# Attention of a two-layer block: values stationary in two column halves, row sums inverted, spread and multiplied across three steps of the next tile

## The reference

```python
s_win = jnp.einsum('bnqgrd,bnkgd->bngrqk', qb, kw).astype(jnp.float32) * scale
s_win = jnp.where(valid[None, :, None, None], s_win, NEG_INF)
s_ctx = jnp.einsum('bnqgrd,bcgd->bngrqc', qb, k_ctx).astype(jnp.float32) * scale
p = jax.nn.softmax(jnp.concatenate([s_win, s_ctx, s_sink], axis=-1), axis=-1).astype(v.dtype)
o = (jnp.einsum('bngrqk,bnkgd->bnqgrd', p[..., :kw_len], vw)
     + jnp.einsum('bngrqc,bcgd->bnqgrd', p[..., kw_len:-1], v_ctx))
...
x = x + g1 * (jnp.concatenate([att, ret, cnv], axis=-1) @ w_out[l])
```

## Time and profile before

| | us |
|---|---|
| median of 3 runs | 1916.67 (1910.70 to 1926.17) |
| the profiled execution, device time | 1919.19 |
| its span, first to last instruction | 1917.4 |
| PE busy, share of the span | 1822.6, 95% |
| DVE / ACT / POOL busy | 1339.3 / 1050.9 / 119.9 |
| DMA | 472.85 MB, mean 247 GB/s |
| mean granted TensorE clock | 0.982 |

### The profile page before, as it was taken

How to read it: one execution, slowest core, us unless ns; L and a number is a source line. 1 busy time by engine, 2 the same in 40 slices (tenths; PEclk the granted TensorE clock), 3 DMA queues, 4 the chain that set the end, 5 groups by cost and what they waited for, 6 DMA issues and landing times.

```text
span 1917.4 us, 23772 instructions
## 1 busy us (share of the span) xinstructions
PE 1822.6 (95%) x8964; PEld 1480.7 (77%) x8964; DVE 1339.3 (70%) x1280; ACT 1050.9 (55%) x1009; POOL 119.9 (6%) x126
## 2 busy tenths in 40 slices
PE   4999899999999999987999999999999999999996
PEld 2986578888888888576888788888888888888885
DVE  2579645333323367756888888889888898898886
ACT  3334644322222153545777776777776776777774
POOL 1123600000000012400000000000000000000000
PEclk8999989999999999997999999999999999999999
DMA  8325823532342234735999999999999999999994
GB/s 291 126 88 207 303 75 78 140 96 86 95 109 83 74 97 132 258 138 175 370 332 354 358 340 345 368 346 354 369 328 362 351 361 359 338 354 352 353 367 154
DMA packets 245911, 472.85 MB, mean 247 GB/s; under 512 B 10546, under 2 KB 60564, under 8 KB 245804
## 3 DMA queue, kind: packets, MB, share of 16 engines
q1 hardware_dynamic: 241712, 468.14, 68.9%
q10 hardware_dynamic: 4092, 3.20, 0.6%
HBM read 470.26 MB, written 1.05 MB: 246 GB/s over the span
## 4 chain that ended last, share of the span: by engine, by line
PE 48%; DMA 21%; DVE 16%; ACT 8%; issue 5%; POOL 2%; SPq 0%; DVEq 0%; ACTq 0%; POOLq 0%
PE bank L543 13%; PE bank L545 13%; PE bank L544 13%; DMA raw<-in_moe_w_gate_dram 10%; DVE parts L1707 9%; ACT parts L1409 6%; DMA raw<-in_moe_w_down_dram 5%; DMA raw<-in_moe_w_up_dram 4%; DMA raw<-in_ada_w_dram 2%; PE bank L561 1%; PE bank L1047 1%; POOL gb L1663 1%; DVE parts L1692 1%; PE bank L790 1%; DVE ACC L2180 1%
## 5 line engine op out<-in xcount | busy, mean ns | idle before, releaser
L1707 DVE TENSOR_TENSOR parts<-raw,parts 128x2048 fp32r<-128x2048 f32 x336 | 764.9, 2289 | 115.0 <-ACT parts L1409 113.9
L1409 ACT ACTIVATE parts<-raw 128x2048 fp32r<-128x2048 f32 x336 | 642.7, 1919 | 260.4 <-DMA raw<-in_moe_w_up_dram 94.9
L543 PE MATMUL bank<-parts,XEr 128*128 128x512 f32 x896 | 357.2, 399 | 8.7 <-DVE parts L1707 6.3
L545 PE MATMUL bank<-parts,XEr 128*128 128x512 f32 x896 | 350.1, 391 | 0.0
L544 PE MATMUL bank<-parts,XEr 128*128 128x512 f32 x896 | 349.4, 390 | 0.0
L1270 ACT ACTIVATE parts<-raw 128x2048 fp32r<-128x2048 f32 (+1 forms) x62 | 113.2, 1831 | 270.2 <-PE bank L545 250.0
L1692 DVE TENSOR_TENSOR parts<-raw,parts 128x2048 fp32r<-128x2048 f32 (+1 forms) x62 | 135.8, 2194 | 138.2 <-ACT parts L1270 137.9
L543 PEld LDWEIGHTS bank<-parts,XEr 128*128 128x128 f32 x896 | 168.7, 188 | 49.9 <-DVE parts L1707 10.3
L545 PEld LDWEIGHTS bank<-parts,XEr 128*128 128x128 f32 x896 | 168.5, 188 | 36.6
L544 PEld LDWEIGHTS bank<-parts,XEr 128*128 128x128 f32 x896 | 168.9, 188 | 32.6
L543 PE MATMUL bank<-parts,HTr 128*128 128x512 f32 x448 | 175.6, 392 | 1.3 <-DVE HTr L1707 0.8
(11 more groups left out here) (245 smaller groups left out, 2289.7 us busy)
## 6 DMA issues: line engine op xcount, KB each, us to landing
raw<-in_moe_w_gate_dram SPq DMA_DIRECT2D x112, 1024.0 KB, 7.2
raw<-in_moe_w_up_dram SPq DMA_DIRECT2D x112, 1024.0 KB, 7.2
raw<-in_moe_w_down_dram SPq DMA_DIRECT2D x112, 1024.0 KB, 6.7
raw<-in_ada_w_dram SPq DMA_DIRECT2D x28, 1024.0 KB, 8.0
more<-in_ada_w_dram SPq DMA_DIRECT2D x20, 1024.0 KB, 7.7
raw<-in_w_in_dram SPq DMA_DIRECT2D x12, 1024.0 KB, 5.1
raw<-in_ffn_w_gate_dram SPq DMA_DIRECT2D x22, 512.0 KB, 4.0
raw<-in_ffn_w_up_dram SPq DMA_DIRECT2D x22, 512.0 KB, 5.4
```

The source lines that it names most:

```text
L543: nc.tensor.matmul(out, st[0], mv[0], start=start, stop=False)
L545: return nc.tensor.matmul(out, st[1], mv[0], start=False, stop=stop)
L1409: nc.scalar.activation(parts[:, n % PARTS, 0, :], raw[:, r, :], ACT.Copy).then_inc(hi_ready, 1)
L1707: return nc.vector.tensor_tensor(out, a, b, op)
```

## The change

- `values`: the values (64 columns of group g) are stationary and write to the partitions 64g to 64g+63 of OB; the turned probabilities are moving (128 columns). The two groups alternate. The result is feature-major: no turn of the attended tile is needed, and `turn_attended` is gone.
- The row sums: VectorE adds the sink and inverts (`invert_sums`) in the next tile's step m % 4 == 0, and for the last tile at the top of step `last`. TensorE spreads them over 64 partitions a group (`spread_sums`, 8 matmuls against the identity) at the top of step m % 4 == 1. ScalarE copies that bank to `proj` (`sums_out`). VectorE multiplies OB by it (`normalise`) at the top of step m % 4 == 2, the last tile's at the end.
- In steps m % 4 == 2 the modulation products run ahead of the values.
- ScalarE and VectorE read the attended tile from `proj` for the high and low parts.
- The first half of each w_out item group is loaded with its rows permuted, as two loads of 64 partitions.

```diff
@@ loads
-                for k0, k1 in HALVES:
-                    split_item([cols(io["w_out"][layer], h * SLICE, (h + 1) * SLICE, k0, k1)],
-                               k1 - k0, SLICE, n % 2, (n + layer) % 2)
+                w = io["w_out"][layer][:, h * SLICE:(h + 1) * SLICE]
+                groups = [w[256 * g:256 * g + 256, :].rearrange("(r p) n -> p r n", p=HEAD_DIM) for g in range(KV_HEADS)]
+                split_item(groups, KT // 2, SLICE, n % 2, (n + layer) % 2)
@@ TensorE
+            def spread_sums(layer, i):
+                t = order_of(layer)[i]
+                mixed[layer, t, 0] = len(mixed) + 1
+                b = open_a(("sums", layer, t))
+                after(recip_ready)
+                turn = i % 2
+                for r in range(4):
+                    for g in range(KV_HEADS):
+                        head = g * 4 + r
+                        mm = nc.tensor.matmul(b[64 * g:64 * g + 64, r * P:(r + 1) * P],
+                                              rsum[:, turn, head:head + 1].broadcast_to([P, HEAD_DIM]), ident, start=True, stop=True)
+                mm.then_inc(a_full, 1)
...
-                    for kb in range(first, NT):
-                        mm = nc.tensor.matmul(OB[:, head * 64:(head + 1) * 64], PT[:, n % 4, kb * P:(kb + 1) * P],
-                                              proj[:, kb, C_V + 64 * g:C_V + 64 * g + 64],
-                                              start=(kb == first), stop=(kb == NT - 1))
+                    for kb in range(first, NT):
+                        for g in range(KV_HEADS):
+                            mm = nc.tensor.matmul(OB[64 * g:64 * g + 64, r * P:(r + 1) * P], proj[:, kb, C_V + 64 * g:C_V + 64 * g + 64],
+                                                  PT[:, (2 * m + g) % 4, kb * P:(kb + 1) * P],
+                                                  start=(kb == first), stop=(kb == NT - 1))
...
                 for m in range(last + 2):
+                    if m % 4 == 1 and m >= 5:
+                        spread_sums(layer, m // 4 - 1)
                     if m < last:
                         scores(2 * m)
                         scores(2 * m + 1)
...
                     if m >= 2:
-                        values(2 * m - 4)
-                        values(2 * m - 3)
-                    if m % 4 == 2 and 6 <= m < last:
-                        turn_attended(layer, order_of(layer)[m // 4 - 1])
-                    if m < last:
+                        if m % 4 == 2 and m < last:
+                            for _ in range(ADA_ITEMS[layer][m]):
+                                ada_product()
+                        values(m - 2)
+                    if m < last and m % 4 != 2:
                         for _ in range(ADA_ITEMS[layer][m]):
                             ada_product()
@@ ScalarE
+            def attended_high(layer, i):
+                t = order_of(layer)[i]
+                act.wait_ge(att_read, evacuated(layer, i))
+                nc.scalar.activation(hTr[:, 0, 0:4, t * P:(t + 1) * P],
+                                     proj[:, t, C_Q:C_RQ].rearrange("p (k n) -> p k n", k=4), ACT.Copy).then_inc(mix_hi, 1)
...
+                    if m % 4 == 1 and m >= 5:
+                        sums_out(m // 4 - 1)
...
+                sums_out(last // 4 - 1)
@@ VectorE
+                def invert_sums(i):
+                    after(esink_ready)
+                    sums = rsum[:, i % 2, :]
+                    step(tt(sums, sums, esink[:, i % 2, :], ALU.add))
+                    nc.vector.reciprocal(sums, sums).then_inc(recip_ready, 1)
+
+                def normalise(i):
+                    tile = order_of(layer)[i]
+                    dve.wait_ge(att_done, base + 8 * i + 8)
+                    dve.wait_ge(a_done, job[("sums", layer, tile)] + 1)
+                    tt(proj[:, tile, C_Q:C_RQ], OB[:, :], proj[:, tile, C_Q:C_RQ], ALU.mult).then_inc(att_read, 1)
...
                 for m in range(last + 2):
+                    if m % 4 == 2 and 6 <= m < last:
+                        normalise(m // 4 - 1)
+                    if m == last:
+                        invert_sums(m // 4 - 1)
...
+                        if m % 4 == 0 and m:
+                            invert_sums(m // 4 - 1)
...
-                    if m % 4 == 1 and m >= 5:
-                        turn = (m // 4 - 1) % 2
-                        tile = order_of(layer)[m // 4 - 1]
-                        after(esink_ready)
-                        step(tt(rsum[:, turn, :], rsum[:, turn, :], esink[:, turn, :], ALU.add))
-                        step(nc.vector.reciprocal(rsum[:, turn, :], rsum[:, turn, :]))
-                        dve.wait_ge(att_done, base + 2 * m - 2)
-                        tt(proj[:, tile, C_Q:C_RQ].rearrange("p (h d) -> p h d", d=HEAD_DIM), OB[:, :].rearrange("p (h d) -> p h d", d=HEAD_DIM),
-                           per_group(rsum[:, turn, :], HEAD_DIM), ALU.mult).then_inc(att_read, 1)
+                    if m == last + 1:
+                        normalise(last // 4 - 1)
```

More of the change, by code:

```diff
@@ L368, in order_of, with evacuated @@
             return (2, 3, 0, 1) if layer == 0 else (0, 1)
+        def evacuated(layer, i):
+            return layer * (NT + 1) + i + 2
         def attention_of(layer):
@@ L780, in turn, with values @@
                     mm.then_inc(a_full, 1)
[L782 to L785, removed]
+                def values(m):
+                    t, r, _ = its[2 * m]
+                    if m % 4 == 0 and m:
                         after(att_read)
-                    pe.wait_ge(a_done, job[("probs", layer, n)] + 1)
                     first = 0 if t < TT else TT
+                    pe.wait_ge(a_done, job[("probs", layer, 2 * m + 1)] + 1)
                     for kb in range(first, NT):
-                        mm = nc.tensor.matmul(OB[:, head * 64:(head + 1) * 64], PT[:, n % 4, kb * P:(kb + 1) * P],
-                                              proj[:, kb, C_V + 64 * g:C_V + 64 * g + 64],
-                                              start=(kb == first), stop=(kb == NT - 1))
-                    mm.then_inc(att_done, 1)
+                        for g in range(KV_HEADS):
+                            mm = nc.tensor.matmul(OB[64 * g:64 * g + 64, r * P:(r + 1) * P], proj[:, kb, C_V + 64 * g:C_V + 64 * g + 64],
+                                                  PT[:, (2 * m + g) % 4, kb * P:(kb + 1) * P],
+                                                  start=(kb == first), stop=(kb == NT - 1))
+                            if kb == NT - 1:
+                                mm.then_inc(att_done, 1)
                 last = len(its) // 2
                 for m in range(last + 2):
+                    if m % 4 == 1 and m >= 5:
+                        spread_sums(layer, m // 4 - 1)
                     if m < last:
@@ L867, in project_out @@
                                     after(att_read)
-                                    turn_attended(layer, tiles[-1])
                                 if i == len(tiles) // 2 - 1:
@@ L1209, in _ @@
                 for j, src in enumerate(srcs):
+                    if src.shape[0] == HEAD_DIM:
+                        sp.dma_start(dst[j * HEAD_DIM:(j + 1) * HEAD_DIM, :, :], src).then_inc(raw_loaded[s], 16)
+                        continue
                     sp.dma_start(dst[:, :, j * part_w:(j + 1) * part_w], src).then_inc(raw_loaded[s], 16)
@@ L1372, in tap, with sums_out @@
                     ins.then_inc(product, 1)
+                def sums_out(i):
+                    copy_out(proj[:, order_of(layer)[i], C_Q:C_RQ], take()[:, :])
                 act.wait_ge(conv_gone, CONV_OUTS * (layer + 1))
@@ L1398, in attention @@
                     if m % 4 == 2 and 6 <= m < last:
-                        mix_high(order_of(layer)[m // 4 - 1], 0)
+                        attended_high(layer, m // 4 - 1)
                     if m == last - 1:
                         split_to(first["out", layer] + 2)
+                sums_out(last // 4 - 1)
             def split_expert(i, n, part):
@@ L1551, in _ @@
                 nc.scalar.activation(gates, CV[:, 0:nt, :], ACT.Silu).then_inc(act_mix, 1)
-                mix_high(order_of(layer)[-1], 0)
+                attended_high(layer, nt - 1)
                 for t in order_of(layer):
```

14 lines of the change are left out of this document (6 added, 8 removed).

## The result

The changed kernel takes 1923.84 us (median of 20 runs, 1915.62 to 1934.15); the kernel before, on the same chip, 1918.06 (20 runs, 1910.35 to 1926.17). The ratio is 1.0037, 95% interval 1.0023 to 1.0051: slower by 4 to 10 us. The forecast was 1.1 us faster. The time lies inside the stated range of 1907 to 1925, but the spread of the runs had set that range, so this says nothing for the mechanism.

The account below looks back on a forecast made before the run. Only the attention stretches of layers 0 and 1 could move, set by TensorE, VectorE/GpSimd, w_out splits and modulation loads in turn. Layer 0's -1.5 and layer 1's +0.4 gave -1.1 us; it said 1915.5 us, range 1907 to 1925.

Parts of the forecast that it names:

- The values block, 0.95: Latent steps: 16 instructions in overlapping column halves take 0.95 us instead of 1.82, saving 0.9 a step.
- Rival (c): Values blocks and spreads: the column halves don't overlap, sum about +13 us, 1930; chance 0.08.
- (d): TensorE blocks: each change of array form drains the engine, sum +1.1 us, 1917.8; chance 0.05.
- A bank that comes free earlier, 0.8: Layer 0, TensorE's wait at 206.54: ScalarE frees the spread's bank sooner, so this turn starts some 0.8 us sooner.
- Layer 0 up to the last scores, "I take -3.5": Layer 0 before scores(14): TensorE's savings count to -4.1 us, taken as -3.5, bounds -1.5 to -4.5.
- Layer 0's end: Layer 0's tail: spread and values wait behind VectorE's split; projection at 258.7 instead of 259.4, -0.7 us.
- "-0.36, -0.4": Layer 0's output projection: -0.36 us for the last turn dropped, 0.4 taken back for a shorter half-clock share.
- Layer 1, "Nothing gained": Layer 1 up to scores(7): saturated modulation loads hold it at 825.5 against 825.59, so no gain.
- "What is hidden": ScalarE's copies fit idle time; layer 1's w_out half loads make the end 1 to 2 us later at most.
- Layer 1's end, +1.05: Layer 1's tail: inversion behind VectorE's split, half-clock spread and values; projection at 841.0 instead of 839.95.
- "-0.4, -0.2": Layer 1's output projection: -0.4 us for the last turn dropped and -0.2 for the clock.
- Rival (b): Both tails: last spread and values stand in series behind VectorE's split, about +2 to +3 us, 1919; chance 0.19.

Follow-up runs that it names:

- e3: Changed kernel with the first half of each w_out group loaded as one load of 128 partitions, rows not permuted; ratio to the kernel before 1.0011 (0.9993 to 1.0030).
- e1: Changed kernel with the last tile's sums inverted in step last-1, ahead of VectorE's w_out split; ratio to the kernel before 1.0019 (0.9999 to 1.0039).
- e15: The kernel of e1 once more, unedited; ratio to the kernel before 1.0033 (1.0007 to 1.0059).
- e2: Changed kernel with ScalarE's copy of the spread's bank ahead of that step's exponentials; ratio to the kernel before 1.0054 (1.0034 to 1.0074).

## Why the prediction was wrong, point by point

- *The values block, 0.95*: right, a little short. 1.03 us, so 0.8 saved in a latent step and not 0.9. The spread takes 1.03 too. Rival (c) is out. So is (d): a values block gives way 0.06 us ahead of its own end with another form behind it.
- *A bank that comes free earlier, 0.8*: right. The turn in step 8 waits for ScalarE's exponential and starts at 206.37, less 0.61 for the entry, against 206.54. But VectorE's maxima and inverted sums, and not TensorE, then set step 9.
- *Layer 0 up to the last scores, "I take -3.5"*: **the first step that failed**. scores(14) comes at 242.70, +0.5 with the entry taken off. I let TensorE's savings run through from step 9 on, and costed the new operations of the other engines at nothing or at idle time. VectorE lost 1.6 us before step 8's maxima (1.1 of it in the low part, whose operand had moved from a bank to SBUF), ScalarE's copy added waits of 0.97 and 1.68 for a bank, and the sums one of 0.86. scores(9) was 1.2 late, and step 10 took another 0.6 more than in the earlier trace rows. The latent steps 11 to 13 did get shorter, 17.1 us for 18.2, with a spread more in step 13. The last scores even come 0.6 us sooner than before, but nobody waits for them: VectorE sets the pace from scores(14) on, and its last maxima are 0.5 us late against the entry, like scores(14), and the split behind them too.
- *Layer 0's end*: right in kind and nearly in size. From scores(14) to the projection the forecast made 20.6 us, it was 20.91. Of the gain that was to pay for it nothing had come. The last turn and the clock, "-0.36, -0.4": the long stage loses 0.8 less than the stage.
- *Layer 1, "Nothing gained"*: **the second step that failed**, by 3.4 us. In "What is hidden" I bounded the w_out loads by their own landing ("the end 1 to 2 us later at most") and took them to stand behind the modulation items. They slowed the last of these: it took 11.7 us to landing and not 9.8. The wait of 2.7 us was then made longer by half clock and by the order that puts the values behind the products. How much of the 3.4 us the loads alone account for stays open: e3 without them takes 3.7 off, but e1 and e15, which keep them, take off 2.7 and 2.8.
- *Layer 1's end, +1.05*: right, 15.67 for 14.36. The "-0.4, -0.2" behind it did not come: +4.7 at the first matmul of the projection, +4.8 at its last. The clock's low stretch only fell later, 857.5 to 860.5.
- Added up, for the long stages: the forecast is -1.1, measured +7.6. The 8.7 between them are 4.3 in layer 0's stage, 3.4 before scores(7), 0.3 in layer 1's tail and 0.7 behind it.
- Rival (b) is the one that came nearest: its mechanism is measured. Its price of 2 to 3 us lacked the loads of layer 1 and VectorE's lost time in layer 0 (+2.8 there by the long stage, where (b) had +0.9).

## What to carry to other kernels

When an operation moves its operand from a bank to SBUF, or a copy is added on an engine that is "idle beside it", look at what that engine does just ahead of the *next* product that the bottleneck waits for, and at who else works in SBUF at that moment. Judge a slower load by what is in flight when it is issued, and not by its own deadline alone. A saving on the engine with the most busy time counts only from the step on in which nothing else sets the pace; before that it turns into a wait, and a long wait costs the clock too.

## What was not expected of the hardware

- A VectorE operation with both inputs in SBUF takes 1.75 us beside GpSimd's additions and 0.68 without (128x512); with one input in a bank it takes 0.68 beside them. The Trainium skill, "SBUF — State Buffer", section "Who interferes with whom", says that a VectorE instruction with two SBUF inputs contends with a GpSimd instruction that reads SBUF, and that one with at most one SBUF input, outside certain fast modes, does not; these rows agree. In the kernel before it could have been read from 206.41, 1.69 us for an operation whose like took 1.23 at 245.57.
- Two loads of 0.5 MB, each on 64 partitions, halve the rate (158 to 231 GB/s for 385) with the DMA engines fully busy, and a load of 1 MB issued 5 us before them lands 3.4 to 5.5 us behind its forerunner instead of 2.6 to 2.7. What TensorE loses by that went from 0.3 to 3.7 us here.
- Column halves give 1.82 to 1.03 us for 16 instructions of 32-bit data.
- Open: e1 and e15 remove 7 to 10 us of the changed kernel's long stages in the profile, and the timed ratio shows 1 to 3.5 us of it at its middle, with wide intervals; e2's ratio is above the changed kernel's. The profiled execution is one of a spread of 15 us, and where the rest of e1's gain goes isn't known. Nor is it explained why layer 1's last item is waited for 0.98 and 1.04 us in e15 and e1 and 2.70 and 3.59 in the two profiles of the changed kernel, whose loads are the same: the runs show only that the w_out loads are issued 0.4 to 2.1 us later after the first scores there.
